# Two feed-forward stages take the norm's factor after their products, with the shift as two moving columns

## What is computed

```python
def rmsnorm_2(x, g):
    y = xf * lax.rsqrt(jnp.mean(xf * xf, axis=-1, keepdims=True) + RMS_EPS)
    return (y * g)
def modulate(h, shift, scale):
    return h * (1 + scale[:, None, :]) + shift[:, None, :]
def swiglu_2(h, w13, w2):
    a, b = jnp.split(h @ w13, 2, axis=-1)
    return (jax.nn.silu(a) * b) @ w2
def second_block(...):
    ...
    for i in range(DEPTH_2):            # 2 layers
        h = modulate(rmsnorm_2(x, norm_g[i, 0]), sh1, sc1)
        x = x + FFN_RES * g1[:, None, :] * swiglu_2(h, ffn_w13[i, 0], ffn_w2[i, 0])
        h = modulate(rmsnorm_2(x, norm_g[i, 1]), sh2, sc2)
        ...                             # mixer
        h = modulate(rmsnorm_2(x, norm_g[i, 2]), sh3, sc3)
        x = x + FFN_RES * g3[:, None, :] * swiglu_2(h, ffn_w13[i, 1], ffn_w2[i, 1])
```

## Time and profile before

| | us |
|---|---|
| median of three runs | 1632.45 |
| lowest, highest | 1630.28, 1633.19 |
| profiled execution, its own time | 1627.3 |
| its span in the trace | 1625.6 |
| TensorE busy | 1611.5 (99%) |
| VectorE busy | 1204.0 (74%) |
| ScalarE busy | 803.2 (49%) |

### The profile page before, as it was taken

The page is one execution under the profiler, slowest core; times in us unless marked ns, Lnnn a source line. Parts: engine busy times, 40 slices in busy tenths (PEclk is TensorE's granted clock), DMA queues, the critical chain, the costliest instruction groups (busy, mean ns, idle before and its releaser), DMA issues.

```text
span 1625.6 us, 33669 instructions
## 1 busy us (share of the span) xinstructions
PE 1611.5 (99%) x14108; PEld 1583.8 (97%) x14108; DVE 1204.0 (74%) x1361; ACT 803.2 (49%) x884; POOL 48.1 (3%) x81
## 2 busy tenths in 40 slices
PE   9999999999999999999999999999999999999998
PEld 9999999999999999999998999999999998899998
DVE  6888886675778878888877788888654568774544
ACT  5443557554644345343557653435434356654342
POOL 0000000000000000000000000000000001000000
PEclk9999999999999999999999999999999999999999
DMA  8998845344568865888643368884555535345551
GB/s 342 338 330 326 304 163 182 131 156 154 195 221 308 297 249 206 329 327 307 250 181 130 130 239 324 302 328 181 207 182 202 185 131 193 145 156 201 188 195 63
DMA packets 51063, 365.01 MB, mean 225 GB/s; under 512 B 5792, under 2 KB 5920, under 8 KB 7072
## 3 DMA queue, kind: packets, MB, share of 16 engines
q1 hardware_dynamic: 40320, 287.04, 48.2%
q0 software_dynamic: 10368, 75.50, 12.8%
q10 hardware_dynamic: 288, 1.18, 0.2%
HBM read 362.65 MB, written 1.05 MB: 224 GB/s over the span
## 4 chain that ended last, share of the span: by engine, by line
PE 94%; DVE 3%; ACT 1%; issue 1%; DVEq 0%; ACTq 0%
PE bank L259 54%; PE bank L295 26%; PE bank L251 3%; PE bank L278 3%; PE bank L2103 1%; PE bank L378 1%; PE bank L389 1%; DVE wlo L190 1%; PE bank L2514 0%; DVE x L321 0%; PE bank L1610 0%; PE bank L2149 0%; DVE xm L453 0%; PE bank L423 0%; PE bank L2055 0%
## 5 line engine op out<-in xcount | busy, mean ns | idle before, releaser
L190 DVE TENSOR_TENSOR wlo<-raw,whi 128x2048 fp32r<-128x2048 f32 x253 | 578.8, 2289 | 205.2 <-ACT whi L182 204.9
L259 PE MATMUL bank<-xh,whi 128*128 128x256 f32 x2608 | 724.8, 278 | 0.8 <-DVE wlo L190 0.8
L259 PE MATMUL bank<-xl,whi 128*128 128x256 f32 x2608 | 721.2, 277 | 0.0
L259 PE MATMUL bank<-xh,wlo 128*128 128x256 f32 x2608 | 721.1, 277 | 0.0
L182 ACT ACTIVATE whi<-raw 128x2048 fp32r<-128x2048 f32 x253 | 483.1, 1913 | 289.4 <-PE bank L259 184.3
L259 PEld LDWEIGHTS bank<-xh,whi 128*128 128x128 f32 x2608 | 490.1, 188 | 2.4 <-DVE wlo L190 1.0
L259 PEld LDWEIGHTS bank<-xl,whi 128*128 128x128 f32 x2608 | 490.1, 188 | 0.1
L259 PEld LDWEIGHTS bank<-xh,wlo 128*128 128x128 f32 x2608 | 489.9, 188 | 0.0
L295 PE MATMUL bank<-hid_hi,whi 128*128 128x256 f32 x1056 | 292.0, 276 | 0.0
L295 PE MATMUL bank<-hid_hi,wlo 128*128 128x256 f32 x1056 | 291.5, 276 | 0.0
L295 PE MATMUL bank<-hid_lo,whi 128*128 128x256 f32 x1056 | 291.5, 276 | 0.0
(11 more groups left out here) (370 smaller groups left out, 1786.6 us busy)
## 6 DMA issues: line engine op xcount, KB each, us to landing
raw<-stream_in SPq DMA_DIRECT2D x269, 1024.0 KB, 4.9
mod_raw<-mod_in POOLq DMA_DIRECT2D x72, 1024.0 KB, 7.6
params<-params_in SPq DMA_DIRECT2D x1, 1474.0 KB, 13.9
x<-x_in SPq DMA_DIRECT2D x2, 512.0 KB, 4.4
raw<-stream_in SPq DMA_DIRECT2D x2, 512.0 KB, 6.5
m_gsu<-sgu_in ACTq DMA_DIRECT2D x1, 1024.0 KB, 7.9
y_out<-x SPq DMA_DIRECT2D x4, 256.0 KB, 2.5
consts<-consts_in SPq DMA_DIRECT2D x1, 280.5 KB, 6.4
```

The source lines that it names most:

```text
L190: dve.tensor_tensor(wlo[:, s, :], raw[:, s, :], whi[:, s, :].bitcast(F32), ALU.subtract)\
L259: last = pe.matmul(out[:, m, :], (whi, wlo)[wp][:, s, k * 256 + m * P:k * 256 + m * P + P], (xh, xl)[ap][:, k, :], start=(k == 0 and j == ...
```

## The change

Stages 7 and 9 get programs of their own, `pe_ffn_shift`, `act_ffn_shift` and `dve_ffn_shift`. As in stage 2, `xh` and `xl` are made of x times the gain without the factor. The shift goes in as two more columns (258 in place of 256) of the moving operand, both the shift's value for the channel; the product's column 256 then holds W s. Each gate and up block now writes two banks, 258 columns of each. VectorE multiplies both banks by the factor, with 1 for the two columns (`rstd_w`), into `gate_s` and `up_s` in SBUF; ScalarE takes the silu with column 256 as bias, in two instructions; VectorE adds the column to the up half and multiplies by the gate, in two instructions. The rows of `xh` and `xl` lie 320 elements apart (1280 bytes) in place of 256, in all stages. The tables of stage 7 now stand after the first turn, between the splits of F0+9 and F0+10. The pair sums behind the residuals of stages 6 and 8 go, and a quarter split of block F0+1 stands there instead. `mod_acc` moves into the shared region, and the banks become one tensor.

```diff
-FACTOR_LATER = (2,)
+SHIFT_LATER = (7, 9)
+FACTOR_LATER = (2,) + SHIFT_LATER
...
-        xh = sb("xh", [P, KD, T], F32R)
-        xl = sb("xl", [P, KD, T], F32R)
+        xh_wide = sb("xh", [P, KD, XW], F32R)
+        xl_wide = sb("xl", [P, KD, XW], F32R)
+        xh, xl = xh_wide[:, :, 0:T], xl_wide[:, :, 0:T]
...
+        def pe_ffn_shift(pe, n, f):
+            xs = (xh_wide[:, :, 0:W], xl_wide[:, :, 0:W])
+            pe.wait_ge(sem("x_updated"), X_STEPS * last_stage(n) + 2)
+            pe_in(pe, F0, FIRST_GATES, first_pass_waits=8 * split_index[n], xs=xs)
+            pe.wait_ge(sem("x_updated"), X_STEPS * last_stage(n) + 4)
+            pe_in(pe, F0 + 1, FIRST_UPS, xs=xs)
+            pe_mean_squares(pe, n)
...
+        def act_ffn_shift(act, n, f):
+            act.activation(xh_wide[:, :, T:W], shift.unsqueeze(2).to_broadcast([P, KD, 2]), ACT.Copy)
+            for b, (k0, k1) in enumerate(X_TILES):
+                act.wait_ge(sem("x_updated"), X_STEPS * (last_stage(n) + 1) - X_STEPS + b + 1)
+                for k in range(k0, k1):
+                    act.activation(xh[:, k, :], x[:, k, :], ACT.Identity, scale=gmod[:, k:k + 1]).then_inc(sem("xn_rounded"), 1)
...
+            act_split(act, F0 + 2)
+            for half in range(2):
+                act_squares(act, half)
+            act_split(act, F0 + 3)
+            act_root(act, n)
+            act_split(act, F0 + 4)
...
+            def silu(s, i=0, ps=0):
+                act.wait_ge(sem("bank_scaled"), L0 + 2 * s + 1 + 2 * ps * i)
+                for m in range(2):
+                    ins = act.activation(gate[:, m, :], gate_s[:, m, 0:T], ACT.Silu, bias=gate_s[:, m, T:T + 1])
...
+        def dve_ffn_shift(dve, n, f):
+            for k in range(KD):
+                dve.wait_ge(sem("xn_rounded"), 8 * split_index[n] + k + 1)
+                if k == 0:
+                    dve.tensor_tensor(xl_wide[:, :, T:W], shift.unsqueeze(2).to_broadcast([P, KD, 2]),
+                                      xh_wide[:, :, T:W].bitcast(F32), ALU.subtract)
+                dve.scalar_tensor_tensor(out=xl[:, k, :], in0=x[:, k, :], scalar=gmod[:, k:k + 1],
+                                         in1=xh[:, k, :].bitcast(F32), op0=ALU.mult, op1=ALU.subtract).then_inc(sem("xn_split"), 1)
+                if k == 3:
+                    dve_split_half(dve, n, 2)
...
+            def post(s, src, block, parity, i=0, per=0, ps=0, between=None):
+                dve.wait_ge(sem("w_used"), block + 1 + per * i)
+                dve.tensor_tensor(up_s[:, :, :], src, over(rstd_w[:, :], [P, 2, W]), ALU.mult).then_inc(sem("bank_scaled"), 1)
...
+                dve.wait_ge(sem("silu_done"), S0 + s + 1 + ps * i)
+                for m in range(2):
+                    ins = dve.scalar_tensor_tensor(out=hid[:, m, :], in0=up_s[:, m, 0:T], scalar=up_s[:, m, T:T + 1],
+                                                   in1=gate[:, m, :], op0=ALU.add, op1=ALU.mult)
...
+            turn(0, True, False)
+            if n == TABLES_AT:
+                dve_tables(dve)
```

More of the change, by code:

```diff
@@ L32 @@
 W = T + 2
+XW = T + 64
 D = 1024
@@ L109, in build_program @@
         mod_raw = sb("mod_raw", [P, 2, BLK])
-        mod_acc = sb("mod_acc", [P, D])
         mod_tab = sb("mod_tab", [P, 144])
@@ L142, in region @@
                 return [here.enter_context(nc.sbuf_tensor(name, shape, dt)) for name, (shape, dt) in tensors.items()]
-        gate, hid, hid_hi, hid_lo, mod_turned, mod_part = region(
+        gate, hid, hid_hi, hid_lo, mod_turned, mod_part, mod_acc, _, gate_s, up_s, rstd_w = region(
             gate=([P, 2, T], F32), hid=([P, 2, T], F32), hid_hi=([P, 2, 2, T], F32R), hid_lo=([P, 2, 2, T], F32R),
-            mod_turned=([P, 32, 32], F32), mod_part=([P, 5, 32], F32))
-        bank = [ctx.enter_context(nc.psum_tensor(f"bank{i}", [P, 512], F32)) for i in range(8)]
+            mod_turned=([P, 32, 32], F32), mod_part=([P, 5, 32], F32), mod_acc=([P, D], F32), mod_gap=([P, P], F32),
+            gate_s=([P, 2, W], F32), up_s=([P, 2, W], F32), rstd_w=([P, W], F32))
+        banks = ctx.enter_context(nc.psum_tensor("bank", [P, 8, 512], F32))
+        bank = [banks[:, i, :] for i in range(8)]
         ACC = bank[0:4]
@@ L236, in build_program, with pe_in @@
         PASSES = ((0, 0), (0, 1), (1, 0))
-        def pe_in(pe, n0, out, i=0, per=0, first_pass_waits=None, beside=None):
+        def pe_in(pe, n0, out, i=0, per=0, first_pass_waits=None, beside=None, xs=None):
             s = slot_of(n0)
+            two_banks = xs is not None
+            xs = (xh, xl) if xs is None else xs
             pe.wait_ge(sem("w_lo_ready"), n0 + 1 + per * i)
@@ L250, in pe_in @@
                             for w in ((whi, wlo) if part == 0 else (whi,)):
-                                last = pe.matmul(out[:, m, :], w[:, s, c:c + P], (xh, xl)[part][:, k, :],
-                                                 start=(part == 0 and k == 0 and m == 0 and w is whi),
+                                last = pe.matmul(out[:, m, :], w[:, s, c:c + P], xs[part][:, k, :],
+                                                 start=(part == 0 and k == 0 and (two_banks or m == 0) and w is whi),
                                                  stop=(part == 1 and k == KD - 1), skip_group_check=True)
@@ L259, in pe_in @@
                         last = pe.matmul(out[:, m, :], (whi, wlo)[wp][:, s, k * 256 + m * P:k * 256 + m * P + P],
-                                         (xh, xl)[ap][:, k, :], start=(k == 0 and j == 0), stop=(k == KD - 1 and j == 2))
+                                         xs[ap][:, k, :], start=(k == 0 and j == 0), stop=(k == KD - 1 and j == 2))
                     if beside is not None and k % 4 == 3 and (m, k) != (1, 7):
@@ L864, in dve_ffn_later, with turn @@
             dve.wait_ge(sem("mod_stored"), 1 + sum(MOD_GROUPS[e] > 0 for e in range(f)))
+        GATES, UPS = banks[:, 4:6, 0:W], banks[:, 6:8, 0:W]
+        FIRST_GATES, FIRST_UPS = banks[:, 0:2, 0:W], banks[:, 2:4, 0:W]
+        def pe_ffn_shift(pe, n, f):
+            F0, S0 = first_block[n], STEPS * f
+            L0 = 2 * STEPS * later_index[n]
+            xs = (xh_wide[:, :, 0:W], xl_wide[:, :, 0:W])
[4 more added lines that the diff above has]
+            pe_mean_squares(pe, n)
+            def turn(i, first):
+                for q in range(2):
+                    b = F0 + 2 + 3 * q
+                    if not (first and q == 0):
+                        pe.wait_ge(sem("bank_scaled"), L0 + 1 + 2 * q + 4 * i)
+                    pe_in(pe, b, GATES, i, 6, xs=xs)
+                    if first and q == 0:
+                        pe.wait_ge(sem("std_ready"), norm_index[n] + 1)
+                        pe_apart(pe, STAT[:, 0:P])
+                    else:
+                        pe.wait_ge(sem("bank_scaled"), L0 + 2 + 2 * q + 4 * i)
+                    pe_in(pe, b + 1, UPS, i, 6, xs=xs)
+                    pe.wait_ge(sem("hid_split"), S0 + 1 + q + 2 * i)
+                    pe_out(pe, b + 2, hid_hi[:, q], hid_lo[:, q], first and q == 0, False, i, 6)
+            turn(0, True)
+            with pe.Fori(1, 5) as i:
+                turn(i, False)
+            pe.wait_ge(sem("hid_split"), S0 + STEPS)
+            pe_out(pe, F0 + 32, hid_hi[:, 0], hid_lo[:, 0], False, True)
@@ new lines, in act_ffn_shift, with round_hidden, turn @@
+        def act_ffn_shift(act, n, f):
+            F0, S0 = first_block[n], STEPS * f
+            L0 = 2 * STEPS * later_index[n]
+            shift = mod_col(*MOD_OF[n])
+            act.wait_ge(sem("gmod_ready"), 2 + sum(m < n for m in MOD_OF))
+            act.activation(xh_wide[:, :, T:W], shift.unsqueeze(2).to_broadcast([P, KD, 2]), ACT.Copy)
[4 more added lines that the diff above has]
+            if n == TABLES_AT:
+                act.dma_start(pos_i[:, :], a_pos).then_inc(sem("pos_loaded"), 16)
+            act_split(act, F0 + 2)
[8 more added lines that the diff above has]
+                    ins = act.activation(gate[:, m, :], gate_s[:, m, 0:T], ACT.Silu, bias=gate_s[:, m, T:T + 1])
+                ins.then_inc(sem("silu_done"), 1)
+            def round_hidden(s, parity, i=0, ps=0):
+                act.wait_ge(sem("hid_ready"), S0 + s + 1 + ps * i)
+                act.activation(hid_hi[:, parity], hid[:, :, :], ACT.Copy).then_inc(sem("hid_rounded"), 1)
+            def turn(i, first, last):
+                for q in range(2):
+                    b = F0 + 2 + 3 * q
+                    if not (first and q == 0):
+                        act_split(act, b + 2, i, 6)
+                    act_split(act, b + 3, i, 6)
+                    silu(1 + q, i, 2)
+                    round_hidden(1 + q, (1 + q) % 2, i, 2)
+                    if not (last and q == 1):
+                        act_split(act, b + 4, i, 6)
+            silu(0)
+            round_hidden(0, 0)
+            turn(0, True, False)
+            if n == TABLES_AT:
+                act_tables(act)
+            more = F0 + 33 < N_BLOCKS
```

(5 more changed lines are left out.)

56 lines of the change are left out of this document (53 added, 3 removed).

## The result

The changed kernel takes 1638.09 us (median of nine runs, 1635.58 to 1640.91) against 1633.12 us (nine runs, 1629.84 to 1634.56). The ratio is 1.0041, with a 95% interval of 1.0032 to 1.0051: 6.7 us slower, where 8.4 us faster was forecast.

A forecast was written before the change was run, and what follows sets the result against it. TensorE, busy 99% of the span, was taken as the bound. Entries -5.7 and -5.5, blocks and loop 0, columns +1.9, tables +0.9 sum to -8.4 us: 1632.45 becomes 1624.0, range 1621.0 to 1630.0.

The forecast's parts named there:

- a slope between two distant sizes: Gate and up blocks of stages 7 and 9: two more columns at 0.9 ns over 2112 matmuls, loss 1.9 us.
- A gain at a stage's entry: TensorE's gaps ahead of F0, the first input block, would go: gain 5.7 us in stage 7, 5.5 in stage 9.

The follow-up runs named there:

- e1: Changed kernel with stages 7 and 9 cut to 256 columns, read and write starting 8 bytes later: 1636.44 us, ratio 1.0019 to the kernel before.
- e3: Changed kernel with the rows of xh and xl 1032 bytes apart in place of 1280: 1687.08 us, ratio 1.0325 to the kernel before.
- e8: Changed kernel with shift columns only in the first four input blocks of stages 7 and 9, rows then made anew: 1622.68 us, ratio 0.9947 to the kernel before.
- e5: Changed kernel with 256 columns from the row's start in stages 7 and 9, the shift's product left out: 1626.23 us, ratio 0.9974 to the kernel before.
- e7: Changed kernel with only the first of three passes 258 columns wide, weights' remainder times shift left out: 1631.65 us, ratio 1.0007 to the kernel before.
- e11: e5 with one pe_apart matmul added ahead of every up block of the loop in stages 7 and 9: 1624.72 us, ratio 0.9961 to the kernel before.
- e4: Changed kernel with the third pass (xl) back at 256 columns, two passes still wide: 1632.16 us, ratio 0.9998 to the kernel before.
- e9: The change in stage 9 alone, stage 7 as in the kernel before: 1635.06 us, ratio 1.0032 to the kernel before.

## What to carry to other kernels

Where an engine is busy to the last percent, price what is added to each of its instructions by a row of that very shape, or take the range as wide as the next dearer shape; a slope between two distant sizes hides a step. Where the operand starts and how far its rows lie apart belong to that shape: e1 and e3 paid without one column more. A gain at a stage's entry of a few us is spent by some ns in two thousand matmuls, so pay for it only as long as it is needed: e8 pays in 8 blocks and not in 44. And a short wait on TensorE may cost more than its length, by the spacing that follows it.

## What the runs showed that I had not expected

- A float32r matmul with 256 moving columns takes 113.3 ns with rows 1024 or 1280 bytes apart, and 120.0 when the read starts 8 bytes later in the row and the write 8 bytes later in the bank. Rows 1032 bytes apart made the whole kernel 3.25% slower than the one before.
- The step past 256 columns: 120.0 to 120.8 ns for 258, 260 and 264.
- Two spacings of the same matmul, 113.3 and 117.8 ns at a granted clock of 1.00. In e5 a wait of 1.0 us was followed by the long one for 23 blocks, and one of 0.78 in e7 by long out blocks to the stage's end; a wait of 0.86 in e11 was not, nor those of 0.15, 0.30 and 0.67 in e8, the changed kernel and e4. So the length of the wait does not decide it. What sets it stays open, as does why stage 9's out blocks have it in the changed kernel, e1 and e9, and not in e4, e5 and e7.
